# Seven block products for queries and keys in a second transformer block, and expert weights read in whole rows

## The reference

```python
# experts: cap = 64 of 512 tokens for each of 16 experts
hid = silu(einsum('becd,edf->becf', xg, w_eg)) * einsum('becd,edf->becf', xg, w_eu)
yo  = einsum('becf,efd->becd', hid, w_ed) * gate[..., None]      # d = 1024, f = 2048
# second block, for each of 2 layers, on x [512, 1024]
h   = rms_norm(x, g_mix[layer])
qkv = h @ w_in[layer]                        # split into q, k, v of three kinds of heads
# q and k are rotated (partial_rope) and go into differential, blocked and dilated attention
x   = x + mix @ w_out[layer]
x   = x + conv_gated_mlp(rms_norm(x, g_ffn[layer]), w_up, conv_w, conv_b, w_down)
```

## Time and profile before

| what | us |
|---|---|
| median of 3 runs | 3653.14 |
| the 3 runs | 3649.88 to 3660.69 |
| the profiled execution | 3648.92 |
| its span in the trace | 3647.1 |
| PE busy | 3426.6 |
| DVE busy | 1630.0 |
| POOL busy | 454.1 |

### The profile page before, as it was taken

How to read it: one execution, slowest core, us unless ns; L and a number is a source line. 1 busy time by engine, 2 the same in 40 slices (tenths; PEclk the granted TensorE clock), 3 DMA queues, 4 the chain that set the end, 5 groups by cost and what they waited for, 6 DMA issues and landing times.

```text
span 3647.1 us, 36445 instructions
## 1 busy us (share of the span) xinstructions
PE 3426.6 (94%) x13712; PEld 1934.2 (53%) x13712; DVE 1630.0 (45%) x3485; ACT 733.3 (20%) x1734; POOL 454.1 (12%) x379
## 2 busy tenths in 40 slices
PE   7999999999999898888888989999999999999999
PEld 4455555445686433233323335556886455568863
DVE  3465666344453203101110114554777645547776
ACT  2144554223102100000000012332000123320001
POOL 0013334011000000000000001101331021013310
PEclk9999999999999899999999999999999999999999
DMA  8433333122223899999999992102223421022233
GB/s 294 174 82 93 104 91 92 41 65 89 81 93 151 320 414 414 414 410 414 414 414 410 414 400 88 35 24 93 93 82 138 142 90 35 24 93 93 92 133 115
DMA packets 288114, 661.57 MB, mean 181 GB/s; under 512 B 33034, under 2 KB 146298, under 8 KB 271558
## 3 DMA queue, kind: packets, MB, share of 16 engines
q1 hardware_dynamic: 226014, 615.35, 44.8%
q10 hardware_dynamic: 61928, 43.89, 4.5%
HBM read 650.66 MB, written 12.34 MB: 182 GB/s over the span
## 4 chain that ended last, share of the span: by engine, by line
PE 71%; DMA 19%; DVE 4%; ACT 2%; SPq 2%; issue 1%; POOL 1%; DVEq 0%; ACTq 0%; POOLq 0%
PE psum L3291 13%; PE psum L308 11%; PE psum L1664 9%; DMA arena<-in_w_exp_gate_dram 7%; DMA arena<-in_w_exp_up_dram 7%; PE psum L3255 6%; PE psum L819 6%; PE psum L2740 5%; DMA arena<-in_w_exp_down_dram 5%; PE psum L2102 5%; PE psum L1488 2%; PE psum L1516 2%; PE psum L1497 2%; PE psum L2015 2%; PE psum L3333 2%; SPq L277 1%
## 5 line engine op out<-in xcount | busy, mean ns | idle before, releaser
L2740 PE MATMUL psum<-arena 128*64 128x512 f32 x3056 | 686.9, 596 | 126.1 <-DMA arena<-in_w_exp_up_dram 64.6
L2740 PEld LDWEIGHTS psum<-arena 128*64 128x64 f32 x3056 | 232.4, 136 | 561.1 <-issue 541.3
L3291 PE MATMUL psum<-arena 128*128 128x256 f32 x2240 | 484.6, 378 | 0.0
L308 PE MATMUL psum<-arena 128*128 128x512 f32 (+1 forms) x1312 | 475.2, 514 | 9.3 <-DVE arena L445 5.4
L3291 PEld LDWEIGHTS psum<-arena 128*128 128x128 f32 x2240 | 423.2, 189 | 61.0
L308 PEld LDWEIGHTS psum<-arena 128*128 128x128 f32 x1312 | 244.0, 190 | 222.8 <-issue 198.1
L1664 PE MATMUL psum<-arena 128*128 128x512 f32 x768 | 342.7, 600 | 0.0
L3255 PE MATMUL psum<-arena 128*128 128x512 f32 x616 | 265.6, 592 | 0.8 <-DVE arena L3523 0.8
L3400 POOL TENSOR_SCALAR arena<-arena 128x512 f32<-128x512 f32 x88 | 181.2, 2068 | 587.8 <-DVE arena L3461 322.6
L819 PE MATMUL psum<-arena 128*128 128x512 f32 (+1 forms) x704 | 241.8, 501 | 1.1 <-DVE arena L556 1.1
L1664 PEld LDWEIGHTS psum<-arena 128*128 128x128 f32 x768 | 143.9, 191 | 186.4 <-issue 184.9
(11 more groups left out here) (349 smaller groups left out, 3738.6 us busy)
## 6 DMA issues: line engine op xcount, KB each, us to landing
arena<-in_w_exp_gate_dram SPq DMA_DIRECT2D x128, 1024.0 KB, 18.6
arena<-in_w_exp_up_dram SPq DMA_DIRECT2D x128, 1024.0 KB, 18.5
arena<-in_w_exp_down_dram SPq DMA_DIRECT2D x126, 1024.0 KB, 22.6
arena<-in_w_in_dram SPq DMA_DIRECT2D x64, 1024.0 KB, 5.4
arena<-in_w_up_dram SPq DMA_DIRECT2D x88, 512.0 KB, 5.4
arena<-in_w_down_dram SPq DMA_DIRECT2D x44, 1024.0 KB, 4.9
arena<-in_w_ada_dram SPq DMA_DIRECT2D x24, 1024.0 KB, 9.8
arena<-acs_scratch ACTq DMA_DIRECT2D x64, 256.0 KB, 5.8
```

Of the source, the lines that this page charges most:

```text
L308: mm = pe.matmul(shaped(b, l, r), l, r, start=kt == 0, stop=kt == nkt - 1)
L2740: mm = pe.matmul(banks[n][64 * j:64 * j + 64, :], lhs[:, kt, 64 * j:64 * j + 64], w, start=kt == 0, stop=kt == 2 * nkb - 1)
L3291: mm = pe.matmul(b, q_weight(L, p, k, kt), q_tokens(k, kt), start=kt == 0, stop=kt == 3)
```

## The change

**Experts.** A block of gate or up weights is now 128 whole rows of 2048 columns (8 KB each): rows 2p + k of 256 rows, for k = 0 or 1. `pe_wide` keeps four banks open and runs through all 2048 columns for each block pair, gate first, then up. The bytes, the number of blocks and the products are as before. Both transposes of the first half (`pe_hidden_turn(pe, m, 0)`) come after the last up product, where the first had come after the gate products of s = 1. The gathered tokens are ordered to fit, by a stationary operand read with a step of two.

**Queries and keys of groups 1 to 3.** In both layers each matrix (256 output columns, 512 tokens, depth 1024) is split into halves three ways. Seven products of blocks replace eight: each is four PE products of 256 columns, so 28 of 256 columns in place of 16 of 512. POOL forms three sums of weight blocks and one difference in place (`pool_qk_sums`, four operations of 512 elements a partition). DVE forms four sums of token blocks once a layer (`dve_token_sums_2`). The seven results are put together by one ACT copy, one DVE operation in `dve_qk_early` and four in `dve_qk_late`; the rotation then reads the sum in SBUF, and the two ACT copies of 512 columns go. DVE keeps the three operations of each rotation, but later in its list.

**Slots and plan.** The block sums take the space of four of the seven slots of the second block, so projections load through three slots (0 to 2). SP waits for the last key product and the last rotation before it loads `w_out`. The end of PLAN2 is redistributed, with the same number of fillers.

A rotation gave its place to the putting together of the first seven products and comes later. The diff, its core:

```diff
+                        c = 256 * (kt // 2)
+                        mm = pe.matmul(b[:, (kt - a) * 128:(kt - a + 1) * 128], r3(h2[:, i, c:c + 256], 2)[:, :, kt % 2], Pb[:, i, :], start=i == 0, stop=i == 3)
...
-            for s in range(2):
-                for wn, w in (("g", A["w_exp_gate"]), ("u", A["w_exp_up"])):
-                    for kb in range(4):
-                        for j in range(2):
-                            block((("e", m, s, wn, j), kb), w[2 * m + j], kb * 256, s * 1024)
+            for wn, w in (("g", A["w_exp_gate"]), ("u", A["w_exp_up"])):
+                for kt in range(8):
+                    for j in range(2):
+                        if m == 0:
+                            sp_once(sp, next(blocks))
+                        rows = w[2 * m + j][256 * (kt // 2):256 * (kt // 2) + 256, :].rearrange("(p k) n -> p k n", k=2)
+                        sp_block(sp, (("e", m, wn, j), kt), 1, 2048, rows[:, kt % 2, :].unsqueeze(1))
...
+        def pe_wide(pe, m, wn):
+
+            banks = [open_bank(pe, (("hid", m, wn), c), PALL) for c in range(4)]
+            for kt in range(8):
+                for j in range(2):
+                    pe.wait_ge(*at("wfull", (("e", m, wn, j), kt)))
+                for c in range(4):
+                    for j in range(2):
+                        w = W.of((("e", m, wn, j), kt))[:, 512 * c:512 * c + 512]
+                        mm = pe.matmul(banks[c][64 * j:64 * j + 64, :], xgb[:, kt, 64 * j:64 * j + 64], w, start=kt == 0, stop=kt == 7)
+                        keys = [("wfree", (("e", m, wn, j), kt))] if c == 3 else []
+                        if kt == 7 and j:
+                            keys.append(("full", (("hid", m, wn), c)))
+                        if keys:
+                            mm.then_inc(*up(S("pe_pair"), *keys))
+                yield kt
...
+            for kt in pe_wide(pe, m, "g"):
+                if m == 0 and kt in (1, 3):
+                    pe_gather(pe, 0, (1 if kt == 3 else "b",))
+                    pe.wait_ge(*at("xgs", 0, 1 if kt == 3 else "b"))
+                elif kt == 3:
+                    pe.wait_ge(*at("xgs", m, 1))
+            if m == 7:
+                pe_scatter(pe, 6)
+            run(pe_wide(pe, m, "u"))
+            pe_hidden_turn(pe, m, 0)
...
-            dve_hidden(dve, m, 0)
+            for s in range(2):
+                dve_hidden(dve, m, s)
             dve_hidden_turn(dve, m, 0)
-            dve_hidden(dve, m, 1)
...
+        QKS = [r3(sb(DSLOT + 2 * WSLOT + 1024 * t, 1024), 256) for t in range(4)]
+        QKT = [r3(WR[:, 4 * WSLOT + 512 * t:4 * WSLOT + 512 * t + 512], 128) for t in range(3)]
+        RAW = [r3(sb(PB + 4096 + 6144 + 3072 + 6656, 3072), 1536)[:, :, 0:512], r3(WR[:, 3 * WSLOT:3 * WSLOT + 1024], 512)]
+
+        def qk_block(L, n, x, h, right):
+
+            return r3(W.of(((("q2", "k2")[x], L, n), 0)), 256)[:, 4 * h:4 * h + 4, 128 * right:128 * right + 128]
...
+        def pe_qk_product(pe, L, n, x, k, b, *keys):
+            w = {1: qk_block(L, n, x, 0, 0), 2: qk_block(L, n, x, 1, 0), 3: qk_block(L, n, x, 1, 1), 4: QKT[2], 5: QKT[0], 6: QKT[1], 7: qk_block(L, n, x, 0, 1)}[k]
+            r = {1: HT2[:, 0:4, 0:256], 2: HT2[:, 4:8, 0:256], 3: QKS[2], 4: HT2[:, 4:8, 256:512], 5: QKS[0], 6: QKS[1], 7: QKS[3]}[k]
+            for kt in range(4):
...
+        def pe_qk_pairs(pe, L, n, pool):
+            left, right = slice(0, 256), slice(256, 512)
+            for x in range(2):
+                nm, u = (("q2", "k2")[x], L, n), (L, n, x)
+                b = open_bank(pe, ("k1", u), pool)
+                pe.wait_ge(*at("wfull", (nm, 0)))
+                pe_qk_product(pe, L, n, x, 1, b[:, left], ("full", ("k1", u)))
+                b = open_bank(pe, ("k26", u), pool)
+                pe_qk_product(pe, L, n, x, 2, b[:, left])
+                pe.wait_ge(*at("KT", u, 6))
+                pe.wait_ge(*at("KS", L, 2))
+                pe_qk_product(pe, L, n, x, 6, b[:, right], ("full", ("k26", u)))
+                yield
+                b = open_bank(pe, ("k45", u), pool)
+                pe.wait_ge(*at("KT", u, 4))
+                pe_qk_product(pe, L, n, x, 4, b[:, left])
+                pe_qk_product(pe, L, n, x, 5, b[:, right], ("full", ("k45", u)))
+                b = open_bank(pe, ("k73", u), pool)
+                pe.wait_ge(*at("KT", u, 7))
+                pe.wait_ge(*at("KS", L, 4))
+                pe_qk_product(pe, L, n, x, 7, b[:, left])
+                pe_qk_product(pe, L, n, x, 3, b[:, right], ("full", ("k73", u)), ("wfree", (nm, 0)))
...
+            pool.wait_ge(*at("wfull", (nm, 0)))
+            if (n, x) != (1, 0):
+                pool.wait_ge(*at("full", ("k45", (L, n, 0) if x else (L, n - 1, 1))))
+            pool.tensor_tensor(QKT[0], b12, b11, ALU.subtract).then_inc(*up(v))
+            pool.wait_ge(*now(v))
+            pool.tensor_tensor(QKT[1], b22, QKT[0], ALU.subtract).then_inc(*up(v, ("KT", u, 6)))
+            pool.wait_ge(*now(v))
+            pool.tensor_tensor(QKT[2], b21, QKT[1], ALU.subtract).then_inc(*up(v, ("KT", u, 4)))
+            pool.tensor_tensor(b12, b22, b12, ALU.subtract).then_inc(*up(v, ("KT", u, 7)))
...
+            dve.tensor_tensor(QKS[0], far[0], far[1], ALU.add).then_inc(*up(v, ("KS", L, 1)))
+            dve.wait_ge(*at("KS", L, 1))
+            dve.tensor_tensor(QKS[1], QKS[0], near[0], ALU.subtract).then_inc(*up(v, ("KS", L, 2)))
+            dve.tensor_tensor(QKS[3], near[0], far[0], ALU.subtract).then_inc(*up(v))
+            dve.wait_ge(*at("KS", L, 2))
+            dve.tensor_tensor(QKS[2], near[1], QKS[1], ALU.subtract).then_inc(*up(v, ("KS", L, 4)))
...
+        def dve_qk_early(dve, L, n, x):
+            u, v, d = (L, n, x), S("dve_quad"), RAW[x]
+            dve.wait_ge(*at("full", ("k26", u)))
+            dve.wait_ge(*at("kc1", u))
+            dve.tensor_tensor(d[:, :, 0:256], r3(PS.of(("k26", u)), 256), rep(d[:, 1, 0:256], 2), ALU.add).then_inc(*up(v, ("free", ("k26", u)), ("k6", u)))
+
+        def act_qk_copy(act, L, n, x):
+            u = (L, n, x)
+            act.wait_ge(*at("full", ("k1", u)))
+            for r in (2 * x, 2 * x + 1) if n > 1 else (2, 3):
+                act.wait_ge(*at("roped", rope2(L, max(n - 1, 0), r)))
+            act.activation(RAW[x][:, 1, 0:256], PS.of(("k1", u))[:, 0:256], ACT.Copy, bias=0.0, scale=1.0).then_inc(*up(S("act_raw"), ("free", ("k1", u)), ("kc1", u)))
+
+        def dve_qk_late(dve, L, n, x):
+            u, v, d = (L, n, x), S("dve_quad"), RAW[x]
+            near, far = d[:, 1, 0:256], d[:, 1, 256:512]
+            four, seven = ("k45", u), ("k73", u)
+            dve.wait_ge(*at("k6", u))
+            dve.wait_ge(*at("full", seven))
+            dve.tensor_tensor(far, PS.of(seven)[:, 0:256], near, ALU.add).then_inc(*up(v, ("k2", u)))
+            dve.wait_ge(*at("full", four))
+            dve.tensor_tensor(near, PS.of(four)[:, 256:512], near, ALU.add).then_inc(*up(v, ("k12", u)))
+            dve.wait_ge(*at("k2", u))
+            dve.tensor_tensor(d[:, :, 256:512], r3(PS.of(four), 256), rep(far, 2), ALU.add).then_inc(*up(v, ("free", four)))
+            dve.wait_ge(*at("k12", u))
+            dve.tensor_tensor(near, PS.of(seven)[:, 256:512], near, ALU.add).then_inc(*up(v, ("free", seven), ("raw", rope2(L, n, 2 * x)), ("raw", rope2(L, n, 2 * x + 1))))
...
+            if n == 1:
+                dve_token_sums_2(dve, L)
+            yield
+            dve_qk_early(dve, L, n, 0)
+            yield
+            dve_qk_late(dve, L, n, 0)
+            yield
+            dve_qk_early(dve, L, n, 1)
+            dve_rope_2(dve, L, n, 0)
+            yield
+            dve_rope_2(dve, L, n, 1)
+            dve_qk_late(dve, L, n, 1)
+            dve_v_2(dve, L, n, 0)
+            yield
+            dve_rope_2(dve, L, n, 2)
+            yield
+            dve_rope_2(dve, L, n, 3)
+            dve_v_2(dve, L, n, 2)
+            yield
+            yield
 
         def pool_proj_2(pool, L, n):
-            for r in range(4):
-                pool_rope(pool, rope2(L, n, r), tmp2[r % 2], ROPES[GROUPS[n][3]][0])
-                yield
-            yield from idle(4)
+            if n == 0:
+                for r in range(4):
+                    pool_rope(pool, rope2(L, n, r), tmp2[r % 2], ROPES[GROUPS[n][3]][0])
+                return
+            if n == 1:
+                pool_qk_sums(pool, L, 1, 0)
+            yield
+            yield
+            pool_qk_sums(pool, L, n, 1)
+            yield
+            pool_cos_2(pool, L, n, 0)
+            yield
+            if n < 3:
+                pool_qk_sums(pool, L, n + 1, 0)
+            yield
+            pool_cos_2(pool, L, n, 1)
+            yield
+            yield from idle(2)
...
-        PLAN2 = [1, 0] * 4 + [1, 1, 0, 0, 1, 1, 0, 1] + [1] * 11 + [0] + [0, 1] * 4 + [1] * 9
+        PLAN2 = [1, 0] * 4 + [1, 1, 0, 0, 1, 1, 0, 1] + [1] * 11 + [1, 1, 0, 1, 0, 1, 0, 0, 0] + [1] * 9
...
```

(11 more changed lines are left out.)

59 lines of the change are left out of this document (27 added, 32 removed).

## The result

The changed kernel takes 3694.46 us (3691.30 to 3697.68, 4 runs) beside 3652.17 us before: a ratio of 1.0110, with a 95% interval of 1.0094 to 1.0126. The prediction was 3658 us, 3634 to 3676. The profiled execution took 3697.68 us, its span is 3695.8 us, 48.7 more than that of before.

What follows compares the result with a forecast made beforehand. Experts were taken as bound by DMA bytes, attention's group 0 by the DVE, ACT and POOL chain, the rest by PE. From the profiled 3648.92, -15.5 for experts and +20 for attention gave 3653.4, so 3658 us, range 3634 to 3676.

Steps and rivals of the forecast that it cites:

- groups 2 and 3: Attention behind group 0, PE the bound: shorter products save 6.7 us, bank waits and plan end take some back, -1.7 a layer.
- sixteenth unit: End of group 0: PE is last again and its filler falls from 8.77 to 5.2 us, -2.0 if the low clock recurs.
- 1. start, token sums: Attention start: four DVE token sums, with POOL's weight sums beside them, delay the first score by 2.5 us.
- 3. bank, then GpSimd's sum: Fifth unit: PE waits for a bank `dve_qk_late` frees, then its sixth product for POOL's second sum, +3.4 us.
- 4. early addition, rotation: Group 0: `dve_qk_early`, and the rotation's last addition waiting for a cosine product after the sixth unit's scaling, +1.4 us.
- 5. late additions: Group 0: the four operations of `dve_qk_late` take 1.65 us from start to start, +1.7 us.
- 6. value tile, four sums: Group 0: value tile 1 waits for a bank; POOL's four sums stand between scalings 8 and 9, then cosine products, +1.9 us.
- upper bound: Attention, per layer: PE's lower clock and POOL's neighbour cost on every DVE pair operation, at most +18 us.
- C: Slower by GpSimd: POOL's sums and DVE's pair operations take turns in group 0, +17.5 us a layer, 3673 us; chance 21%.
- A: The cover holds: DVE's added attention operations fall in its waits for PE, 0 a layer, 3638 us; chance 12%.
- B: PE is the bound everywhere: 26 us from queries and keys plus 15.5 from experts off, 3612 us; chance 8%.
- D: Whole expert rows don't load faster, the rate stays at 410 GB/s, 3674 us; chance 8%.

Runs made afterwards that it cites:

- the run apart: Expert part of the change alone on the kernel before, queries and keys as before: 3636.75 us beside 3654.04, ratio 0.9953.
- e_oldend: The changed kernel with the end of the plan (PLAN2) as before, so group 3's value tiles stand again one between each two units: 3693.34 us.

## Why the prediction was wrong

**What held.** The experts are bound by their bytes: -15.5 predicted, -16.9 in the trace, -17.3 by the run apart. Part of that nearness is luck: a pair gained 0.17 us and not 0.15, which would be 19.0 over 112 pairs, and the stop before the down products, priced at 1.3, cost nothing at m = 7 (TensorE stopped 0.95 us, and the second pair of down blocks came on the old beat). Where the other 2 us went was not looked for. MLP, first network, and loads through three slots cost nothing: no row of TensorE in the attention waits for a DMA.

**What failed: attention, +10 a layer, where it was +29.6 and +27.3.** The ledger of layer 0, measured between VectorE's first score rows (L1596) of the units, each from the first projection's start; the first is the 2244.21 above, and "groups 2 and 3" is all behind the sixteenth unit:

| step | predicted | measured |
|---|---|---|
| 1. start, token sums | +2.5 | +5.3 |
| 2. first bank | +1.0 | +0.8 |
| 3. bank, then GpSimd's sum | +3.4 | +4.2 |
| 4. early addition, rotation | +1.4 | +2.6 |
| 5. late additions | +1.7 | +2.0 |
| 6. value tile, four sums | +1.9 | +3.6 |
| 7. fourth rotation | +2.0 | +2.1 |
| sixteenth unit | -2.0 | +0.4 |
| groups 2 and 3 | -1.7 | +8.7 |
| sum | +10.2 | +29.6 |

- **Steps 1, 4 and 6 were mis-sized by GpSimd, 5.7 us.** The prediction took the 1.10 against 0.69 us of one multiply as the price of GpSimd beside it, though it said that only half of it overlapped; the whole overlap costs about a GpSimd operation for each of VectorE's. It had the right rule at hand: the Trainium skill, "SBUF — State Buffer", section "SBUF: two separate sides", calls the shared port pair an exclusive lock; by it step 1 was to be +6, and it measured +5.3. Step 1 falls to +0.9 with the weight sums cut. Steps 4 and 6 are held by the cosine products, whose pair made a rotation's two operations 2.0 us longer in each; the run without these products shows step 6 at +1.7 and step 4 at +1.9. The weight sums together cost 17.0 us over both layers and the cosine products 6.0 more, part of which the kernel before pays too.
- **The credit at the sixteenth unit.** Its 2.0 us are 7.15 less 5.2, with the low clock costing the same 1.6 us again. It cost more: TensorE had now stopped for 3.28 us, not 2.75, and the three rows behind took 0.87, 2.08 and 7.88 us, where the same work at full clock takes 0.49, 1.13 and 5.45. That is 3.8 us in place of the 1.6.
- **Groups 2 and 3 were taken as TensorE-bound, with room for VectorE's additions: the largest error, 10.4 us.** A matrix there, in TensorE's rows of group 3:

```profile
2382.23 5.45 PE L3004 MATMUL psum<-arena 128*128 128x256 f32 x24
2387.52 0.60 PE L1497 MATMUL psum<-arena 128*128 128x128 f32 x4
...
2389.11 7.19 PE L3004 MATMUL psum<-arena 128*128 128x256 f32 x32
2396.14 0.82 PE L1497 MATMUL psum<-arena 128*128 128x128 f32 x6
```

  That is 5.29 + 7.03 = 12.32 us from start to start for 28 products. A wide piece is 6.98 from start to start, where the prediction took its busy 7.15; so a matrix saves 1.64 us, not 2.17, and four save 6.6. Behind the sixteenth unit's filler 4.4 of it are left. But TensorE's waits in this part rose from 2.6 to 11.5 us (the sum over its rows in order of time), and the clock behind them took some 4.2: together +8.7. The prediction had counted the bank waits about right (4.0 with the means product, 3.7 measured), and valued the plan's end at +0.6 where from L1516 at 2412.65 on it was +7.6. The old end would have cost as much (`e_oldend`): it is VectorE's list, longer by its additions (5.7 us of this part in the traces of layer 0) and held by GpSimd's cosine products (3.4). VectorE was half idle in the earlier trace rows, yet in these units its list is what is late.
- **The upper bound** of +18 a layer stopped short for the same reason: it had nothing for VectorE's list as the bound of groups 2 and 3.

Of the rivals, C was the nearest in kind, with its 21%: its mechanism is shown, at no more than 11.5 us a layer (8.5 + 3.0, with GpSimd's own lateness and the clock in it) beside its 7.5 over a count that had some of it already. It gave 3673, since it shared the count of the rest. A and B had the wrong sign, and D fell with the 421 GB/s. None of them had VectorE's own additions as the largest term.

**The 57.7 us of the projections by the runs:** GpSimd's sums 17.0, its cosine products 6.0, VectorE's additions 20.7, and 14.0 for all that is left: token sums, list order, banks and clock, less the 19.7 that TensorE saves (12 matrices at 1.64). Each kernel set against the kernel before of its own call gives 18.9, 4.7, 20.3 and 15.7. How the last term splits was not tried.

## What to carry to other kernels

Fewer TensorE columns bought with additions on VectorE and GpSimd were a loss here, where their lists already followed TensorE closely: the additions themselves on VectorE cost as much as GpSimd's turns with it. Where both engines run two-input operations on SBUF side by side, count about one whole operation of the other for each. Count a stop of TensorE with the low clock behind it, and test each of several lates apart, since removing one only shows the next. In a stage bound by DMA look at the packets first: whole rows of 8 KB took 0.5% off this kernel without any change of its arithmetic.

## What the runs showed of the hardware

- VectorE's additions that read PSUM were not held by GpSimd's sums (0.68 us at 2288.57), while two-input SBUF operations were, and so was the fp32 scaling with a single SBUF input (0.73 us became 2.78). The Trainium skill, "SBUF — State Buffer", section "Who interferes with whom", lists `tensor_scalar` among the operations that can take the shared pair; the trace agrees.
- GpSimd's own scalings (L1653) held nothing: a two-input multiply of VectorE inside one took its 0.69 us. Only beside GpSimd's two-input operations was VectorE slower, in the whole attention of layer 0. VectorE, then GpSimd:

```profile
2286.57 0.69 DVE L1683 TENSOR_TENSOR arena<-arena 128x512 f32<-128x512 f32 x1
...
2288.57 0.68 DVE L3080 TENSOR_TENSOR arena<-psum,arena 128x512 f32<-128x512 f32 x1
```

```profile
2285.98 1.56 POOL L1653 TENSOR_SCALAR arena<-arena 128x512 f32<-128x512 f32 x1 [3.43 <-DVE arena L1586]
2287.51 1.61 POOL L3039 TENSOR_TENSOR arena<-arena 128x512 f32<-128x512 f32 x1
2289.20 1.27 POOL L3041 TENSOR_TENSOR arena<-arena 128x512 f32<-128x512 f32 x1
```

- Expert weights came at 421 GB/s with all rows of 8 KB and at 412 with gate and up in rows of 4 KB, with the same order and slots. Halving the transfers from 1 MB to 512 KB at rows of 4 KB changed nothing (5.13 and 5.12 us a pair).
- Behind stops of 3.89 and 4.78 us the first 3.73 us of TensorE's work took 5.41 to 6.26 us in both layers of the changed kernel. Behind the stop of 3.28 us the clock was at its lower level too (0.50 of full from 2317.44 to 2320.25).
